# Transposing h of chunk 0 on TensorE instead of through scratch memory, in a two-layer macaron encoder

## What is computed

```python
D_MODEL = 1024; SEQ = 256; DEPTH = 2; D_FF = 2816

def _swiglu(h, w_in, w_out):
    gu = h @ w_in
    gate, up = jnp.split(gu, 2, axis=-1)
    return (jax.nn.silu(gate) * up) @ w_out

def reference(x, ...):
    for l in range(DEPTH):
        x = x + 0.5 * _swiglu(_rmsnorm(x, ffn1_norm[l]), ffn1_w_in[l], ffn1_w_out[l])
        ...
        x = x + jnp.concatenate([out_a, out_b], axis=-1) @ w_mix_out[l]
        x = x + 0.5 * _swiglu(_rmsnorm(x, ffn2_norm[l]), ffn2_w_in[l], ffn2_w_out[l])
    return x
```

## Time and profile before

| what | us |
|---|---|
| median of 3 runs | 913.63 |
| lowest and highest | 912.89, 919.4 |
| the profiled execution, its own time | 915.78 |
| its span, from first to last instruction | 914.0 |
| busy in it: TensorE (PE) | 895.2 |
| VectorE (DVE) | 561.6 |
| ScalarE (ACT) | 448.2 |

### The profile page before, as it was taken

How to read it: one execution, slowest core, us unless ns; L and a number is a source line. 1 busy time by engine, 2 the same in 40 slices (tenths; PEclk the granted TensorE clock), 3 DMA queues, 4 the chain that set the end, 5 groups by cost and what they waited for, 6 DMA issues and landing times.

```text
span 914.0 us, 12202 instructions
## 1 busy us (share of the span) xinstructions
PE 895.2 (98%) x4230; PEld 736.3 (81%) x4230; DVE 561.6 (61%) x758; ACT 448.2 (49%) x522; POOL 56.0 (6%) x115
## 2 busy tenths in 40 slices
PE   8699999999999999999999999999999999999998
PEld 7488888888778788888887888888877878888887
DVE  5464655657977555555566565555779666565562
ACT  5444434447856354444444544444578454354340
POOL 3400000103100000000020000000111000000000
PEclk9899999999999999999999999999999999999999
DMA  8678877854265687767637777676433757687731
GB/s 281 190 253 237 258 215 251 247 196 138 94 207 168 225 263 224 261 205 236 215 106 248 250 234 264 218 240 192 136 134 117 252 160 255 218 261 234 251 138 47
DMA packets 150722, 190.05 MB, mean 208 GB/s; under 512 B 9268, under 2 KB 124280, under 8 KB 150688
## 3 DMA queue, kind: packets, MB, share of 16 engines
q1 hardware_dynamic: 149216, 186.55, 63.0%
q0 software_dynamic: 1296, 2.92, 1.4%
q10 hardware_dynamic: 176, 0.14, 0.0%
HBM read 176.72 MB, written 12.84 MB: 207 GB/s over the span
## 4 chain that ended last, share of the span: by engine, by line
PE 85%; DVE 6%; DMA 4%; ACT 3%; SPq 1%; issue 1%; POOL 0%; ACTq 0%; DVEq 0%; POOLq 0%
PE U L1148 10%; PE U L1151 10%; PE U L1149 10%; PE TR L1151 6%; PE TR L1149 6%; PE TR L1148 6%; PE C L1148 6%; PE C L1151 6%; PE C L1149 6%; PE D L1148 5%; PE D L1149 5%; PE D L1151 5%; DMA h_rows<-qs 2%; DVE w_lo L792 2%; DVE sc L997 1%
## 5 line engine op out<-in xcount | busy, mean ns | idle before, releaser
L792 DVE TENSOR_TENSOR w_lo<-raw,w_hi 128x2048 fp32r<-128x2048 f32 x150 | 340.8, 2287 | 98.0 <-ACT w_hi L556 97.5
L556 ACT ACTIVATE w_hi<-raw 128x2048 fp32r<-128x2048 f32 x150 | 283.6, 1908 | 43.7 <-DMA raw<-in_ffn_w_in_dram 37.5
L1148 PE MATMUL U<-w_hi,xT 128*128 128x512 f32 (+1 forms) x448 | 172.9, 386 | 0.0
L1151 PE MATMUL U<-w_hi,xT 128*128 128x512 f32 (+1 forms) x448 | 171.1, 382 | 0.0
L1149 PE MATMUL U<-w_lo,xT 128*128 128x512 f32 (+1 forms) x448 | 171.1, 382 | 0.0
L586 ACT ACTIVATE hT_hi<-gv 128x256 fp32r<-128x256 f32 x80 | 29.0, 410 | 199.8 <-DMA gv<-h_rows 199.8
L1148 PE MATMUL TR<-w_hi,xT 128*128 128x512 f32 x320 | 124.6, 389 | 0.0
L1151 PE MATMUL TR<-w_hi,xT 128*128 128x512 f32 x320 | 124.5, 389 | 0.0
L1149 PE MATMUL TR<-w_lo,xT 128*128 128x512 f32 x320 | 124.5, 389 | 0.0
L829 DVE TENSOR_TENSOR hT_lo<-gv,hT_hi 128x256 fp32r<-128x256 f32 x80 | 30.4, 422 | 114.0 <-ACT hT_hi L586 114.0
L1148 PEld LDWEIGHTS U<-w_hi,xT 128*128 128x128 f32 x448 | 84.2, 188 | 16.5
(11 more groups left out here) (160 smaller groups left out, 974.3 us busy)
## 6 DMA issues: line engine op xcount, KB each, us to landing
raw<-in_ffn_w_in_dram SPq DMA_DIRECT2D x168, 512.0 KB, 5.5
raw<-in_ffn_w_out_dram SPq DMA_DIRECT2D x88, 512.0 KB, 4.2
raw<-in_w_mix_in_dram SPq DMA_DIRECT2D x28, 512.0 KB, 4.7
h_rows<-qs SPq DMA_DIRECT2D x40, 256.0 KB, 4.0
gv<-h_rows SPq DMA_DIRECT2D x160, 64.0 KB, 1.9
raw<-in_w_mix_out_dram SPq DMA_DIRECT2D x16, 512.0 KB, 3.7
raw<-in_ffn_w_in_dram SPq DMA_DIRECT2D x16, 256.0 KB, 4.7
bias<-bias_rows POOLq DMA_DIRECT2D x8, 192.0 KB, 3.9
```

The source lines that it names most:

```text
L556: act.activation(w_hi[:, p % SLOTS, :], raw[:, p % RAW, :], ACT.Copy).then_inc(hi_ready, 1)
L792: dve.tensor_tensor(w_lo[:, p % SLOTS, :], raw[:, p % RAW, :], w_hi[:, p % SLOTS, :].bitcast(F32), ALU.subtract).then_inc(lo_ready, 1)
L1148: pe.matmul(out_, x_hi, w_hi[:, slot, c], start=start, stop=False, skip_group_check=reopened)
L1151: last = pe.matmul(out_, x_lo, w_hi[:, slot, c], start=False, stop=stop, skip_group_check=reopened)
```

## The change

Chunk 0 is now treated nearly as chunk 10 is. VectorE multiplies it in plain order, TensorE transposes it with four instructions in its chunk 1, behind the two `enter` with u = 0, into C1 (token tile 0) and D1 (token tile 1). These two banks of the output sums are not in use until the first `leave`. ScalarE and VectorE take hT_hi and hT_lo from them, each in its order behind the split of chunk 0's output weights, and the first `leave(0, t)` waits for the rest of its own token tile only. Chunk 0's transpose on VectorE, its store, loads and conversions are gone. Chunks 1 to 9 go through the scratch tensor as before. SP's loop now begins at chunk 2; its order is otherwise the same.

```diff
@@ -205,6 +205,7 @@
         PV, SG = acc[1][1], U[1]
+        HT = {0: [C1, acc[1][1]], 10: TR}
@@ -310,10 +311,11 @@
         def n_turned(L, f, c, j=0):
-            return L * (2 * (NCH - 1)) + j * 2 + ((NCH - 1) * f + c + 1)
-
-        def n_hT(L, f, t):
-            return L * 4 + (2 * f + t + 1)
+
+            return L * (2 * (NCH - 2)) + j * 2 + ((NCH - 2) * f + c)
+
+        def n_hT(L, f, c, t):
+            return L * 8 + (4 * f + (2 if c == 10 else 0) + t + 1)
@@ -416,16 +418,15 @@
                 def chunk(c, j=0):
                     load_in(L, f, c + 1, 0, j)
                     load_in(L, f, c + 1, 1, j)
-                    store_h(L, f, c - 1, j)
-                    load_h(L, f, c - 1, j)
+                    if c >= 2:
+                        store_h(L, f, c - 1, j)
+                        load_h(L, f, c - 1, j)
                     load_out(L, f, c, j)
-                load_in(L, f, 1, 0)
-                load_in(L, f, 1, 1)
-                load_out(L, f, 0)
+                chunk(0)
+                chunk(1)
                 with sp.Fori(0, 4) as j:
-                    chunk(1, j)
                     chunk(2, j)
-                chunk(9)
+                    chunk(3, j)
                 load_out(L, f, 10)
@@ -575,10 +576,10 @@
-            def take_hT(L, f, t):
-                act.wait_ge(hT_psum, n_hT(L, f, t))
+            def take_hT(L, f, c, t):
+                act.wait_ge(hT_psum, n_hT(L, f, c, t))
                 act.activation(hT_hi[:, 0, :, t * P:(t + 1) * P],
-                               TR[t][:, 0:FC].rearrange("p (k n) -> p k n", k=2), ACT.Copy).then_inc(hT_hi_done, 1)
+                               HT[c][t][:, 0:FC].rearrange("p (k n) -> p k n", k=2), ACT.Copy).then_inc(hT_hi_done, 1)
@@ -607,7 +608,8 @@
                 def chunk(c, j=0):
                     split(L, pos_in(f, c + 1, 0), j)
-                    round_h(L, f, c - 1, j)
+                    if c >= 2:
+                        round_h(L, f, c - 1, j)
                     split(L, pos_in(f, c + 1, 1), j)
@@ -623,6 +625,8 @@
                 split(L, pos_out(f, 0))
+                take_hT(L, f, 0, 0)
+                take_hT(L, f, 0, 1)
                 chunk(1)
@@ -806,7 +810,7 @@
-                if c == 10:
+                if c in (0, 10):
                     dve.scalar_tensor_tensor(out=h[:, t, :], in0=up, scalar=0.5, in1=silu_, op0=ALU.mult, op1=ALU.mult
                                              ).then_inc(h_done, 1)
                     return
@@ -902,7 +906,8 @@
                 def chunk(c, j=0):
                     split(L, pos_in(f, c + 1, 0), j)
-                    rest_h(L, f, c - 1, j)
+                    if c >= 2:
+                        rest_h(L, f, c - 1, j)
                     if L == 0 and f == 0 and c == 1:
@@ -918,13 +923,13 @@
                 if L == 0 and f == 0:
                     multiply(L, f, 0, 1)
-                    turn_h(L, f, 0)
                     split(L, pos_in(f, 1, 1))
                 else:
                     split(L, pos_in(f, 1, 1))
                     multiply(L, f, 0, 1)
-                    turn_h(L, f, 0)
                 split(L, pos_out(f, 0))
+                take_hT(L, f, 0, 0)
+                take_hT(L, f, 0, 1)
                 chunk(1)
@@ -1269,14 +1274,14 @@
-                def transpose_h(t):
-                    pe.wait_ge(h_done, n_ffn(L, f, 10, t))
+                def transpose_h(c, t):
+                    pe.wait_ge(h_done, n_ffn(L, f, c, t))
                     for kk in range(2):
-                        last = pe.transpose(TR[t][:, kk * P:(kk + 1) * P], h[:, t, kk * P:(kk + 1) * P], ident[:, :])
+                        last = pe.transpose(HT[c][t][:, kk * P:(kk + 1) * P], h[:, t, kk * P:(kk + 1) * P], ident[:, :])
                     last.then_inc(hT_psum, 1)

                 def leave(c, t, j=0, stop=False):
-                    pe.wait_ge(hT_lo_done, n_ffn(L, f, c, t if c == 10 else 1, j))
+                    pe.wait_ge(hT_lo_done, n_ffn(L, f, c, t if c in (0, 10) else 1, j))
@@ -1291,6 +1296,9 @@
                             enter(c, t, u, j)
+                        if c == 1 and u == 0:
+                            transpose_h(0, 0)
+                            transpose_h(0, 1)
```

More of the change, by code:

```diff
@@ L637, in ffn @@
                     split_rest(L + 1, 0)
-                take_hT(L, f, 0)
+                take_hT(L, f, 10, 0)
                 if after is not None:
@@ L644, in ffn @@
                 silu(L, f, 10, 1)
-                take_hT(L, f, 1)
+                take_hT(L, f, 10, 1)
                 if after is None and L == DEPTH - 1:
@@ L830, in rest_h, with take_hT @@
                                       h_as_tokens(hT_hi[:, c % 2, kk, :]).bitcast(F32), ALU.subtract).then_inc(hT_lo_done, 1)
-            def take_hT(L, f, t):
-                dve.wait_ge(hT_hi_done, n_ffn(L, f, 10, t))
+            def take_hT(L, f, c, t):
+                dve.wait_ge(hT_hi_done, n_ffn(L, f, c, t))
                 cols = slice(t * P, (t + 1) * P)
-                dve.tensor_tensor(hT_lo[:, 0, :, cols], TR[t][:, 0:FC].rearrange("p (k n) -> p k n", k=2),
+                dve.tensor_tensor(hT_lo[:, 0, :, cols], HT[c][t][:, 0:FC].rearrange("p (k n) -> p k n", k=2),
                                   hT_hi[:, 0, :, cols].bitcast(F32), ALU.subtract).then_inc(hT_lo_done, 1)
@@ L1319, in ffn @@
                 enter(10, 1, 0)
-                transpose_h(0)
+                transpose_h(10, 0)
                 enter(10, 1, 1)
                 leave(9, 0)
-                transpose_h(1)
+                transpose_h(10, 1)
                 leave(10, 0)
```

## The result

| | before | changed |
|---|---|---|
| median, us (4 runs each) | 916.51 | 903.62 |
| lowest to highest | 912.89 to 919.53 | 903.41 to 905.03 |
| profiled execution, own time | 915.78 | 903.41 |
| its span | 914.0 | 901.6 |

The ratio is 0.9864, with a 95% interval from 0.9816 to 0.9913: the change makes the kernel 1.4% faster. The spans differ by 12.4 us, where 15.8 were forecast. The runs of the kernel before lie 6.6 us apart, those of the changed one 1.6.

What follows compares the result with a forecast made beforehand. TensorE, busy 98% of the span, bounds the kernel; only its idle time, slow stretches or work count. −18.2 + 1.9 + 0.5 = −15.8 us, from 913.63 to 897.8 us; range 896.0 to 904.0.

Steps and rivals of the forecast that it cites:

- Chunk 0's waits: TensorE's waits at the first product into C, leave(0, 0), in four blocks, with slow products after: 18.20 us to go.
- Why block 1 waited so long: Block 1, chunk 0: h's store stands in SP's queue behind chunk 2's loads until 28.33; ScalarE gets data at 40.87.
- The transposes: 16 added on TensorE, eight pairs at 0.24 us each between products: 1.9 us added.
- The bound of 4.4: Upper end for the 16 added transposes on TensorE: 0.272 us each as if nothing overlapped, 4.4 us.
- The gain copy in block 1: VectorE's copy ends TensorE's gain_taken wait at about 33.5, leave comes at 33.9: 0.4 us to spare.
- The next trip: Chunk 1's h through memory, block 1: hT_lo finished at 50.2, TensorE there at 50.3; estimated wait 0.5 us.
- the 3.5 that I gave as the upper end: Most for chunk 1's wait in block 1: 1.8 us waiting plus 1.7 of slow products.
- what I subtracted: From span to median time: the profiled execution's 2.15 us above the median of the runs, taken over to the forecast.
- rival A: The wait moves to chunk 1 of block 1: 3.5 us, time 900.8, or 903.3 with dearer transposes; chance 0.17.
- the forecast's own case: Chunk 0's waits gone, about 0.5 us wait at chunk 1 of block 1: span 898.2, time 897.8 us; chance 0.68.
- Rival C: Block 1, leave(c, 0) for chunks 1 to 9: every trip late, 3.5 us each, 31.5 in all, 929; chance 0.03.
- Rivals B and D: B: weights can't follow in block 1, 905.5, chance 0.07; D: gain_taken still holds TensorE, 907 to 912 us, chance 0.05.

## Why the prediction was right or wrong

**Chunk 0's waits (18.20 us in the sum).** Right, and well sized: blocks 1 to 4 gave 11.44, 3.22, 0.58 and 1.14 us against 11.35, 3.2, 0.4 and 1.3, transposes included. That half the gain of block 2 and a quarter of that of block 1 was clock, not waiting, held too: these stretches run at 1.00 now. The 0.58 us that block 1 started sooner is luck.

**Why block 1 waited so long.** Half right. I put it on SP's order alone. Holding the bias table's store back took 3.8 us off the wait of 8.7, with SP's order as it was; moving h's store forward, which takes it out of the table's way as well, left 2.0. Both causes act. It didn't matter for the sum, since the change takes the trip away, but it was the hint I passed over: the bias table's traffic can add some 4 us to a trip beside it, and the 9.29 us of chunk 1's trip were read where no table's store was near.

**The transposes (1.9 us).** Right: 0.45 us for four in block 1, which makes 1.8 in all. The bound of 4.4, their own durations added up, is refuted by the run with 32 more.

**The gain copy in block 1 (0.4 us to spare).** It was done at 32.3, TensorE came at 33.3: 1.0 to spare; no cost. The transposes also came 1 us sooner than the 28.0 "at the latest".

**The next trip (0.5 us).** This is the step that failed. The place was right, chunk 1 of block 1. The store, which I had at 39.7, went at 38.04, since the input unit ahead of it came sooner than I had reckoned; with a trip of 9.29 us that would have left no wait at all. Wrong was the sentence that the data follow 9.29 us later, as today. They followed 13.0 us later (38.04 to 51.04), since the store took 9.7 us for 5.2. I had taken over a transfer time from a stretch whose neighbours didn't all move by the same amount, as each hangs on something else. The weights ahead of the store moved up by 8.6 us (40.97 to 32.40) and the store by 9.2, with VectorE. The bias load hangs on TensorE's last product of chunk 0's leave and moved up by 12.0: it lay 3.9 us behind the store before, and now 1.15. The bias table's store, which POOL sends, moved up by only 2.7 (32.83 to 30.15), and so came to lie beside the weights that were now issued at 32.40. With the first bias load later the store took 5.9 to 7.8 us, and with the table's store later too 5.0. The measured 4.52 us (2.77 and 1.75) also lies above the 3.5 that I gave as the upper end: I took it from the longest hT_lo wait in the rows, and a wait at another place has no reason to stop there.

**From the spans to the time.** The forecast was 897.8 us and the median came to 903.62, 5.8 more. Of these, 3.4 are the gain that was too large, nearly all from the step above. Another 2.15 are what I subtracted because the profiled execution of the kernel before was slower than its median. That was no property of the change: of the three runs behind that median two lay at 913 and one at 919, a fourth came to 919.53, and the changed kernel's profiled execution (903.41) stands at its own median. That subtraction should not have been made.

**The rivals.** What happened is rival A, to which I gave 0.17, at 901.6 in span where the forecast had 898.2 and A's price gives 901.2. It named the bias table's store and loads as a reason for, and both had a part in it. With the bias loads out of the way the forecast's own case appears: span 897.1 to 898.5. Rival C, all further trips late, is no fancy: it is what the run with the loads two units later shows, at 17.29 us a chunk and with no change of the transposes. It ran over six chunks, and its price per chunk was far below the 3.5 that I had set, about 1 us, as only some of its waits brought the slow clock. Rivals B and D did not happen.

**The Trainium skill on the trip.** By the fixed 2.0 us plus bytes at 436 GB/s (DMA: Bandwidth & Descriptors, the table of two cost components, given there for transfers sent by GpSimd) the store takes 2.6 us. Here the same 256 KB, sent by SP, took from 2.1 us, when nothing of SP's was issued shortly ahead of it, to 10.0. The rule's figure is near the least that was measured, and no estimate for a transfer among weights.

## What to carry to other kernels

When a stage moves earlier, list for each transfer in it and around it what releases it, and shift each by its own releaser (here by 2.7, 8.6, 9.2 and 12.0 us); transfers that kept apart may meet. A wait taken away shows the next-tightest hand-over of the same kind: compute its slack with transfer times from the busiest stretch, not from the quiet one of before. And place small side loads by trial: here releasing them two units later made the changed kernel some 10 us slower, and three units later 2.5 us faster.

## What the runs showed of the hardware that I had not expected

- One and the same store of 256 KB took 2.1, 4.1, 5.0, 7.0 or 9.7 us from issue to landing, by what stood ahead of it in SP's queue and what POOL's queue sent beside it. That a load issued 1.15 us after the store can hold it up is shown by the six runs where no bias load went out beside this store and the table's store stayed where it was (5.9 to 7.8 us against 9.7 and 10.0); it doesn't always, as the 6.9 us with a load 0.9 us behind show. Through what it acts is not shown. Both landed together at 47.7 us, and from 44 to 48 us little was moved:

```profile
42.00:44.00 2.00, 2.00 (x11) 1.65 (x10) 0.65 (x1) 1.32 (x1) 0.00 (x0) 1.00 1.09 362
44.00:46.00 2.00, 2.00 (x11) 1.65 (x10) 1.64 (x1) 0.00 (x0) 0.00 (x0) 1.00 0.54 77
46.00:48.00 2.00, 2.00 (x10) 1.67 (x9) 0.00 (x0) 0.00 (x0) 0.00 (x0) 1.00 0.13 39
```

- The lower clock doesn't follow from the length of a wait alone. In the run of the kernel before with the bias loads alone later, TensorE waited 1.99 us in block 2 and 1.95 us in block 3; from the first product into C to the next chunk's it then took 18.05 and 16.45 us. The one had some 1.7 us of slow products, the other next to none. In the run with the bias table's store held back as well, the wait in block 2 was longer, 2.21 us, and the next chunk followed after 16.46 us.
